# Rotary half heads exchanged by transfers instead of TensorE, and a down projection that waits by groups

## The chip, the cores and the metric

The program runs on one core of one Trainium2 chip. The metric is the time of one execution on the device in microseconds (us). The kernel before took 3718.03 us, the median of three runs (3717.81 to 3725.36).

Engines are named as the profile names them: PE is TensorE (matrix products), DVE is VectorE, ACT is ScalarE, POOL is GpSimd, SP is SyncE, which here only starts transfers.

## The reference

Sequence length and width are 1024. Two attention layers (the first block) are followed by one layer of another kind (the second block).

```
h = layer(layer(x))            # 1st block: 4 branches of 256 columns each
  a: banded attention, band of 8 chunks of 64, relative bias
  b: latent attention: q, k from rms-normed low-rank projections; 64 plain + 32 rotary dims per head
  c: banded attention, band of 2 chunks; q (4 heads) and k (2 heads) of 64 dims, all rotary
  m: attention to a memory of 256 tokens
  y = concat(branch * silu(gate)) @ w_out;  h = layernorm(alpha*x + y)
x = x + 0.5 * swiglu(rmsnorm(x))            # 2nd block: D_FF = 2816 = 22 tiles of 128
x = x + mixer(rmsnorm(x))
x = x + 0.5 * swiglu(rmsnorm(x))

rope(x):   x1, x2 = split(x, 2)             # the two halves of a head
           [x1*cos - x2*sin, x2*cos + x1*sin]
swiglu(h): g, u = split(h @ w_gu, 2);  (silu(g) * u) @ w_down
```

So a rotary tile needs, beside itself, a copy in which the halves of every head are exchanged. Tiles here lie features by tokens (128 partitions by 1024 columns), so the exchange moves data between partitions, which an elementwise engine does not do inside one operation on 128 partitions.

## The kernel before, in words

**Products.** A projection of 128 output features is a *panel*: SP loads 512 KB of float32 weights (`panel_raw`), POOL splits them into a float16 and a bfloat16 part (`panel_parts`, lines 823 to 825), and PE forms each product of 128x128 by 128x512 as three matmuls (lines 1026 to 1028). Attention scores, transposes and values are plain float32 matmuls, as is the exchange of halves. Each float32 matmul shows as two records.

**Attention layers.** A layer is 48 *slots*: 16 of branch a, 8 of c, 16 of b, 8 of m. Slot n on PE is: scores of slot n+1 (L1196 to L1207), fill 0, transposes (L1219), fill 1, transposes (branches with two groups), fill 2, values of slot n (L1238), fill 3. A fill takes the next steps of a list of dense pieces (`LAYER_FILL`), spread evenly over the four fills of all slots of a branch; one step is one product of 128x512. A position is written `at` = 4 x slot + fill: branch a has 0 to 63, c 64 to 95, b 96 to 159. Meanwhile DVE takes the row maxima of slot n+1, ACT its exponentials, DVE the inverse of the sums, POOL scales the rows (L859), and ACT and DVE copy the transposes out of PSUM (L1543, L1956). Each engine runs its own program in order, at the same positions: `keep_layer(at)` on ACT and DVE empties the PSUM banks of the pieces that end there, `layer_background` on DVE holds the rest (the rms norm chain `normalise`, from two positions after `ss_kv`, and the rotary tables). Dense pieces alternate between two PSUM banks (`dense_ready`, `dense_free`), so PE begins a piece only when the last but one is copied out.

**The exchange.** Ten dense pieces per layer, `swap_cq0`, `swap_cq1`, `swap_ck` (end of branch a), `swap_q` and `swap_k` (middle of branch c), two halves of 512 columns each, multiply the tile by a 128x128 permutation with signs (`swap`, L1077). For each half DVE runs `rotate`: the product from PSUM times sin, the tile times cos, and their sum. After `swap_q` and `swap_k` DVE also copies the 32 rotary rows of each head beside its plain rows (L2016 and L2022, seven copies). The scores of c wait for `rope_c_done`, those of b for `rope_b_done`.

**Feed-forward.** `ffn` runs twice. Eleven turns of four tiles form gate and up; DVE and ACT make each activation tile and DVE splits it (`act_split` counts 22). Then eight tiles of the down projection each sum three groups of 8, 8 and 6 activation tiles (`FF_GROUPS`). Before the first, PE waits once for all 22 (L1341).

## Time and profile before

| | |
|---|---|
| median of the runs | 3718.03 us |
| profiled execution, its own time | 3720.31 us |
| its span | 3718.5 us |
| PE busy in the span | 3462.1 us (93%) |
| DVE, ACT, POOL busy | 1544.2, 1002.5, 1573.3 us |
| mean granted PE clock | 0.978 of full |
| share of PE in the chain that ended last | 85% |

The profile is of one execution. A row of the timeline gives the start, the duration, the engine, the line, the operation with output and inputs, a count, and in brackets the idle time of the engine before it with what ended that. PE's matmuls overlap in the records: back to back 128x512 float16 products start 0.216 us apart at full clock and are shown as 0.38 us long. The two attention layers come first, and the second feed-forward ends the program.

### The profile page before, as it was taken

Reading aid. Unit: us, or ns where it says so; the run is one execution under the profiler, and the core shown is the slowest. Engines: PE = TensorE matmul, PEld = TensorE weight load, DVE = VectorE, ACT = ScalarE, POOL = GpSimd, SP = SyncE. Lnnn points to the kernel's source line nnn. Section 1 sums busy time; section 2 is a strip of 40 time slices with the busy share of each in tenths; the row PEclk is TensorE's granted clock in tenths of the full one; section 3 lists DMA queues with packets and bytes.
Section 4 is the critical chain, followed back from the end, with each engine's and each line's share of the span. In section 5 each row is a group of like instructions: output and inputs, shape, how many; then the busy total and the mean of one; then the engine's idle time right before and its main releaser. Section 6 shows DMA issues by size and latency. Waiting matters only on the chain.

```text
span 3718.5 us, 50039 instructions
## 1 busy us (share of the span) xinstructions
PE 3462.1 (93%) x20022; PEld 1785.2 (48%) x20340; DVE 1544.2 (42%) x2435; ACT 1002.5 (27%) x1744; POOL 1573.3 (42%) x1034
## 2 busy tenths in 40 slices
PE   7988997998999799999987999999998979999999
PEld 4554653645564344444434554555544434444444
DVE  3255347145436733331115455545554463333100
ACT  1433322233332300000002455554554320000000
POOL 4444652444564233332324555645554423333232
PEclk9999999998999999999999999999999999999999
DMA  3100112110021111111121101111011111111112
GB/s 121 41 19 35 60 60 83 46 33 32 23 85 36 34 51 51 51 51 47 52 72 73 47 28 48 48 46 48 27 48 72 45 34 52 50 51 51 48 48 80
DMA packets 52885, 188.33 MB, mean 51 GB/s; under 512 B 6624, under 2 KB 7136, under 8 KB 52192
## 3 DMA queue, kind: packets, MB, share of 16 engines
q1 hardware_dynamic: 51408, 181.08, 13.9%
q10 hardware_dynamic: 1296, 4.72, 0.3%
q8 instruction: 128, 2.10, 0.2%
q14 instruction: 53, 0.43, 0.0%
HBM read 173.20 MB, written 12.58 MB: 50 GB/s over the span
## 4 chain that ended last, share of the span: by engine, by line
PE 85%; DVE 5%; ACT 5%; issue 3%; POOL 1%; DMA 1%; SPq 0%; DVEq 0%; POOLq 0%; ACTq 0%
PE pair L1028 25%; PE pair L1026 24%; PE pair L1027 21%; PE pair L1238 3%; PE pair L1207 2%; PE pair L1460 2%; PE pair L1219 2%; DVE arena L1884 2%; PE pair L1436 1%; PE pair L1419 1%; ACT arena L1804 1%; POOL panel_parts L825 1%; ACT arena L1636 1%; PE pair L1367 1%; PE pair L1046 1%
## 5 line engine op out<-in xcount | busy, mean ns | idle before, releaser
L1026 PE MATMUL pair<-operand,panel_parts 128*128 128x512 f16 x2816 | 1075.6, 382 | 90.4 <-POOL panel_parts L825 61.3
L1028 PE MATMUL pair<-operand,panel_parts 128*128 128x512 f16 x2816 | 1071.7, 381 | 12.2
L1027 PE MATMUL pair<-operand,panel_parts 128*128 128x512 bf16 x2584 | 984.4, 381 | 0.0
L824 POOL TENSOR_SCALAR panel_parts<-panel_raw 128x1024 f16<-128x1024 f32 (+3 forms) x287 | 296.0, 1031 | 1568.1 <-PE pair L1028 1054.5
L825 POOL TENSOR_TENSOR panel_parts<-panel_raw,panel_parts 128x1024 bf16<-128x1024 f32 (+3 forms) x287 | 633.7, 2208 | 23.9
L1026 PE MATMUL pair<-arena,panel_parts 128*128 128x512 f16 (+1 forms) x1216 | 464.4, 382 | 41.1 <-DVE arena L1884 29.6
L1026 PEld LDWEIGHTS pair<-operand,panel_parts 128*128 128x128 f16 x2816 | 276.0, 98 | 440.1 <-issue 143.2
L859 POOL TENSOR_SCALAR arena<-arena,row_inv 128x256 f32<-128x256 f32 (+7 forms) x256 | 338.6, 1335 | 344.2 <-DVE row_inv L1946 343.9
L1028 PE MATMUL pair<-arena,panel_parts 128*128 128x512 f16 (+1 forms) x1216 | 463.7, 381 | 5.4 <-issue 1.1
L1028 PEld LDWEIGHTS pair<-operand,panel_parts 128*128 128x128 bf16 x2816 | 276.7, 98 | 336.5 <-issue 7.2
L1027 PE MATMUL pair<-arena,panel_parts 128*128 128x512 bf16 (+1 forms) x1130 | 429.8, 380 | 0.0
L1027 PEld LDWEIGHTS pair<-operand,panel_parts 128*128 128x128 f16 x2816 | 276.7, 98 | 287.8 <-issue 9.0
L976 POOL TENSOR_SCALAR arena<-arena,row_inv 128x512 f32<-128x512 f32 (+1 forms) x128 | 246.9, 1939 | 184.6 <-DVE row_inv L2411 184.6
L1884 DVE TENSOR_TENSOR arena<-arena 128x1024 f32<-128x1024 f32 (+4 forms) x183 | 233.6, 1276 | 79.6 <-ACT arena L1797 49.3
L1715 ACT ACTIVATE arena<-arena 128x1024 f32<-128x1024 f32 x44 | 46.5, 1057 | 756.7 <-DVE arena L1884 756.7
L1636 ACT ACTIVATE arena<-arena,neg_max 128x256 f32<-128x256 f32 (+7 forms) x256 | 155.8, 609 | 344.6 <-DVE neg_max L1927 344.3
L1884 DVE TENSOR_TENSOR arena<-pair,arena 128x1024 f32<-128x1024 f32 (+2 forms) x64 | 67.6, 1056 | 372.2 <-PE pair L1028 367.2
L1026 PEld LDWEIGHTS pair<-arena,panel_parts 128*128 128x128 f16 x1216 | 119.6, 98 | 206.8 <-issue 46.3
L1887 DVE SCALAR_TENSOR_TENSOR residual<-pair,residual 128x1024 f32<-128x1024 f32 (+1 forms) x32 | 39.1, 1221 | 421.6 <-PE pair L1028 421.4
L1927 DVE CUSTOM_DVE_ANT_0 arena<-pair,arena 128x256 f32<-128x256 f32 (+7 forms) x256 | 133.7, 559 | 192.0 <-PE pair L1207 114.7
L1543 ACT ACTIVATE arena<-pair 128x512 f32<-128x512 f32 (+1 forms) x234 | 136.2, 588 | 281.3 <-PE pair L1028 161.1
L1028 PEld LDWEIGHTS pair<-arena,panel_parts 128*128 128x128 bf16 x1216 | 120.2, 99 | 144.0 <-issue 6.9
(213 smaller groups left out, 4241.4 us busy)
## 6 DMA issues: line engine op xcount, KB each, us to landing
panel_raw<-in_wgu SPq DMA_DIRECT2D x88, 512.0 KB, 3.2
panel_raw<-in_wl SPq DMA_DIRECT2D x58, 512.0 KB, 3.2
panel_raw<-in_wm SPq DMA_DIRECT2D x56, 512.0 KB, 3.3
panel_raw<-in_wdn SPq DMA_DIRECT2D x32, 512.0 KB, 3.2
residual_spill<-residual SPq DMA_DIRECT2D x16, 512.0 KB, 2.9
residual<-residual_spill SPq DMA_DIRECT2D x15, 512.0 KB, 5.9
panel_raw<-in_wl SPq DMA_DIRECT2D x18, 384.0 KB, 2.9
panel_raw<-in_wdn SPq DMA_DIRECT2D x16, 384.0 KB, 2.9
```

Of the source, the lines that this page charges most:

```text
L824: chained(nc.gpsimd.tensor_scalar(WP[:, s, 0, 0:cols], RAW[:, s, 0:cols], HI_MAX, -HI_MAX, ALU.min, ALU.max))
L825: nc.gpsimd.tensor_tensor(WP[:, s, 1, 0:cols].bitcast(LO), RAW[:, s, 0:cols], WP[:, s, 0, 0:cols], ALU.subtract).then_inc(panel_split[s], 1)
L859: nc.gpsimd.tensor_scalar(p, p, RI[:, b:b + 1], None, ALU.mult).then_inc(slot_scaled, 1)
L976: nc.gpsimd.tensor_scalar(p, p, RI[:, b:b + 1], None, ALU.mult).then_inc(mix_scaled, 1)
L1026: nc.tensor.matmul(out, stat[0], mov[0], start=first, stop=False)
L1027: nc.tensor.matmul(out, stat[0], mov[1], start=False, stop=False)
L1028: return nc.tensor.matmul(out, stat[1], mov[0], start=False, stop=last)
L1238: m = nc.tensor.matmul(OUTL[u.h * HD:(u.h + 1) * HD, (i // 2) * P:(i // 2 + 1) * P], v_of(s, u, kt), PTL[g][:, c0:c0 + P], start=j == 0, s ...
L1543: return nc.scalar.activation(dst, src, ACT.Copy, scale=scale)
L1636: nc.scalar.activation(p, p, ACT.Exp, bias=NM[:, b:b + 1], scale=-1.0, accum_out=RS[:, b:b + 1]).then_inc(slot_probs, 1)
L1884: return V_.tensor_tensor(out, a, b, op)
L1927: m = V_.tensor_tensor_reduce(out=probs_of(n, s, u), in0=score_cols(s, u), in1=bias_of(s, u), scale=-1.0, scalar=3e38, op0=ALU.add, op1=AL ...
```

## The change

The ten exchange pieces leave PE's list. Instead ACT, after it has copied the second half of a rotary tile, issues transfers that write the exchanged rows to a second tile (`SWAPPED`): four of 32 rows for each of `cq0`, `cq1`, `ck`, two of 16 rows for the key (`bq1`), eight of 16 rows for the query (`ur`). The sign is now a per-partition scale in the sine table. DVE rotates in three whole-width steps at three successive positions, the first three positions after the piece ends (`ROPE_WAIT`). SP issues seven transfers of 32 rows in place of DVE's seven copies, ahead of the panels of branch b. The remaining pieces are spread anew over the fills: 198 steps in place of 204 over branch a, 52 in place of 56 over branch c. In the feed-forward PE waits before each group for that group's activation tiles alone.

```diff
 LAYER_FILL = {
-    "a": [..., "cq0", "ss_q", "ss_kv", "cq1", "ck", "swap_cq0", "swap_cq1", "swap_ck", "cv", "cg0"],
-    "c": ["ur", "un0", "un1", "cg1", "swap_q", "swap_k", "uk0", "uk1", "uv0", "uv1", "bg0"],
+    "a": [..., "cq0", "ss_q", "ss_kv", "cq1", "ck", "cv", "cg0"],
+    "c": ["ur", "un0", "un1", "cg1", "uk0", "uk1", "uv0", "uv1", "bg0"],
+ROPE_WAIT = (("bq1", 3), ("cq0", 3), ("cq1", 3), ("ck", 3), ("ur", 3))
...
+        SWAPPED = {"cq0": GATES[4], "cq1": GATES[5], "ck": GATES[6], "bq1": GATES[7], "ur": GATES[7]}
+        ROTATED = {"cq0": CQ[0], "cq1": CQ[1], "ck": CK, "bq1": BRAW_K, "ur": UR}
...
 # SP, after the load of mem and before the panels of branch b
+                sp.wait_ge(kv_split, l + 1)
+                sp.wait_ge(rope_k_rotated, l + 1)
+                for h in (0, 2, 3):
+                    sp.dma_start(BK[h][64:96], BK[1][64:96]).then_inc(rope_b_done, 16)
+                sp.wait_ge(rope_q_rotated, l + 1)
+                for h in range(4):
+                    sp.dma_start(BQ[h][64:96], UR[32 * h:32 * h + 32]).then_inc(rope_b_done, 16)
...
 # PE, feed-forward
-                pe.wait_ge(act_split, FT * idx)
                 with pe.Fori(0, 2) as i:
...
                             w = weights(f"down{idx}", i, 3 * j + g)
+                            pe.wait_ge(act_split, FT * (idx - 1) + k0 + nk)
...
 # ACT, keep_layer
+                    if name in SWAPPED and c == 1:
+                        layer_piece_kept(act, name, l)
+                        w = 32 if name[0] == "c" else 16
+                        rows = slice(64, 96) if name == "bq1" else slice(0, P)
+                        if name == "ur":
+                            act.wait_ge(rope_k_rotated, l + 1)
+                        for r in range(rows.start, rows.stop, 2 * w):
+                            for a, b in ((r, r + w), (r + w, r)):
+                                nc.scalar.dma_start(SWAPPED[name][a:a + w], ROTATED[name][b:b + w]).then_inc(swap_loaded[name], 16)
...
 # ACT, rotary tables
-                nc.scalar.activation(sin, sin, ACT.Sin).then_inc(rope_tab, 1)
+                nc.scalar.activation(sin, sin, ACT.Sin, scale=RC[:, 4 + n:5 + n]).then_inc(rope_tab, 1)
...
 # DVE
+            def rotate(l, name, step):
...
+                if step == 0:
+                    dve.wait_ge(rope_tab, 2)
+                    dve.wait_ge(swap_loaded[name], (l + 1) * 16 * {"bq1": 2, "ur": 8}.get(name, 4))
+                    chained(tt(other, other, sin[rows], ALU.mult))
+                elif step == 1:
+                    chained(tt(x, x, cos[rows], ALU.mult))
                 else:
+                    tt(x, x, other, ALU.add).then_inc({"bq1": rope_k_rotated, "ur": rope_q_rotated}.get(name, rope_c_done), 1)
...
 # DVE, layer_background, ahead of normalise
+                for name, wait in ROPE_WAIT:
+                    step = at - kept_at(l, name) - wait
+                    if 0 <= step < 3:
+                        rotate(l, name, step)
```

On PE, in slot 13 of layer 1 (the last rows of piece `ck`, then the exchange of `cq0`, `cq1`, `ck`, with the transposes of the slot between), before:

```order
L1026 MATMUL pair<-operand,panel_parts 128x512
L1027 MATMUL pair<-operand,panel_parts 128x512
L1028 MATMUL pair<-operand,panel_parts 128x512
L1077 MATMUL pair<-arena,swap 128x512 [waits dense_free1,dense_free0] x2
L1219 MATMUL pair<-ident,arena 128x128 [waits slot_kept0,slot_scaled]
L1219 MATMUL pair<-ident,arena 128x128 x3
L1219 MATMUL pair<-ident,arena 128x128 [waits slot_kept1]
L1077 MATMUL pair<-arena,swap 128x512 [waits dense_free1,dense_free0] x4
L1219 MATMUL pair<-ident,arena 128x128 [waits slot_kept0,slot_scaled]
```

Now, at the same transposes, the end of `ck` and the first rows of `cv`:

```order
L1220 MATMUL pair<-ident,arena 128x128 [waits slot_kept0,slot_scaled]
L1220 MATMUL pair<-ident,arena 128x128 x3
L1220 MATMUL pair<-ident,arena 128x128 [waits slot_kept1]
L1036 MATMUL pair<-operand,panel_parts 128x512
L1037 MATMUL pair<-operand,panel_parts 128x512
L1038 MATMUL pair<-operand,panel_parts 128x512
```

The six exchange pieces with their waits on both PSUM banks are gone, and ordinary steps stand there. On DVE in the same slot, after the row maxima (`ISA`), before (`rotate` in six-row groups, one step of the norm chain in between):

```order
L1884 TENSOR_TENSOR arena<-pair,arena 128x512 [waits dense_ready0,rope_tab]
L1884 TENSOR_TENSOR arena<-arena 128x512
L1884 TENSOR_TENSOR arena<-arena 128x512 [waits dense_free0,dve_step]
L1884 TENSOR_TENSOR arena<-pair,arena 128x512 [waits dense_ready1,rope_tab,dve_step]
L1884 TENSOR_TENSOR arena<-arena 128x512
L1884 TENSOR_TENSOR arena<-arena 128x512 [waits dense_free1,dve_step]
L1887 SCALAR_TENSOR_TENSOR residual<-residual,layer_cols 128x1024
L1956 COPY stats<-pair 128x128 [waits slot_values,slot_turned1]
L1946 RECIPROCAL row_inv<-row_sum 128x1 [waits slot_probs] x2
```

Now, from the end of slot 12 (the rotation of `cq1` starts there) into slot 13:

```order
L1894 TENSOR_TENSOR arena<-arena 128x1024 [waits swap_loaded_cq1,rope_tab]
L1897 SCALAR_TENSOR_TENSOR residual<-residual,layer_cols 128x1024 [waits cols_loaded,dve_step]
L1937 ISA arena,neg_max<-pair,arena 128x640 [waits slot_scores]
L1937 ISA neg_max 128x1
L1937 ISA arena,neg_max<-pair,arena 128x640
L1937 ISA neg_max 128x1
L1894 TENSOR_TENSOR arena<-arena 128x1024
L1897 SCALAR_TENSOR_TENSOR residual<-residual,layer_cols 64x1024 [waits dve_step]
L1966 COPY stats<-pair 128x128 [waits slot_values,slot_turned1]
L1956 RECIPROCAL row_inv<-row_sum 128x1 [waits slot_probs] x2
```

One whole-width operation of a rotation stands at each position, beside one step of the norm chain, and none reads PSUM. On ACT at the start of branch c, where `ur` is copied out, the eight transfers stand between those copies and the copies of `un0`:

```order
L1544 ACTIVATE arena<-pair 128x512 [waits slot_values,dense_ready0]
L1544 ACTIVATE arena<-pair 128x512 [waits dense_ready1]
L1635 DMA arena<-arena 16x1024 [waits rope_k_rotated,dense_free1,dense_free0]
L1635 DMA arena<-arena 16x1024 x7
L1544 ACTIVATE residual<-pair 64x512 [waits kv_split,dense_ready0]
```

## Rows read from the trace of the kernel before

**Rows 1.** The page: busy time by engine.
```profile
PE 3462.1 (93%) x20022; PEld 1785.2 (48%) x20340; DVE 1544.2 (42%) x2435; ACT 1002.5 (27%) x1744; POOL 1573.3 (42%) x1034
```

**Rows 2.** Windows: us, busy (x) of PE, PEld, DVE, ACT, POOL; clock, DMA.
```profile
60.00:258.70 198.70, 190.78 (x1349) 109.02 (x1363) 83.21 (x196) 73.02 (x146) 93.53 (x60) 0.98 0.09 31
258.70:352.60 93.90, 74.77 (x437) 40.66 (x445) 46.22 (x145) 36.24 (x101) 42.30 (x38) 0.87 0.10 34
```

**Rows 3.** One of PE's waits, whole span: total us, times, longest.
```profile
PE pair L1077 <- DVE arena L1884: 10.9, 10, 2.3
```

**Rows 4.** The exchange line: count, ns min/median/max, first and last start.
```profile
L1077 PE MATMUL pair<-arena,swap x32: 592/595/1222, 213.1 to 910.9; 128*128 128x512 f32 x32
```

**Rows 5.** Timeline of PE, layer 1, slot 13, the exchange for branch c.
```profile
213.15 1.02 PE L1077 MATMUL pair<-arena,swap 128*128 128x512 f32 x2
...
222.25 2.08 PE L1077 MATMUL pair<-arena,swap 128*128 128x512 f32 x2 [2.32 <-DVE arena L1884]
...
226.35 1.27 PE L1219 MATMUL pair<-ident,arena 128*128 128x128 f32 x5
...
230.92 1.31 PE L1238 MATMUL pair<-stats,arena 128*64 128x128 f32 x20 [0.92 <-DVE stats L1956]
```

**Rows 6.** Timeline of DVE there.
```profile
214.89 3.14 DVE L1884 TENSOR_TENSOR arena<-arena 128x512 f32<-128x512 f32 x2
...
218.67 1.41 DVE L1884 TENSOR_TENSOR arena<-arena 128x512 f32<-128x512 f32 x2
...
232.47 1.22 DVE L1884 TENSOR_TENSOR arena<-residual,arena 128x1024 bf16<-128x1024 f32 x1
```

**Rows 7.** Timeline of POOL there.
```profile
214.62 2.13 POOL L825 TENSOR_TENSOR panel_parts<-panel_raw,panel_parts 128x1024 bf16<-128x1024 f32 x1
```

**Rows 8.** Timeline of PE, layer 1, branch c, values of slots 18 to 21.
```profile
290.34 1.09 PE L1238 MATMUL pair<-stats,arena 128*64 128x128 f32 x16 [1.15 <-ACT stats L1543]
...
292.76 0.93 PE L1207 MATMUL pair<-arena 64*128 64x128 f32 x8
...
298.59 1.09 PE L1238 MATMUL pair<-stats,arena 128*64 128x128 f32 x16 [0.68 <-ACT stats L1543]
...
313.56 0.61 PE L1026 MATMUL pair<-arena,panel_parts 128*128 128x512 f16 x1 [4.45 <-DVE arena L1884]
...
315.64 1.55 PE L1238 MATMUL pair<-stats,arena 128*64 128x128 f32 x12 [0.62 <-issue]
...
326.76 0.23 PE L1026 MATMUL pair<-panel_parts,arena 128*128 128x128 f16 x1 [3.68 <-ACT residual L1543]
...
330.94 1.09 PE L1238 MATMUL pair<-stats,arena 128*64 128x128 f32 x16
```

**Rows 9.** Timeline of DVE there: the gate of a piece.
```profile
301.82 0.69 DVE L1887 SCALAR_TENSOR_TENSOR arena<-arena,pair 128x512 f32<-128x512 f32 x1 [1.68 <-ACT arena L1580]
```

**Rows 10.** Timeline of ACT, start of branch c: copies of `ur`, then of `un0`.
```profile
264.79 1.06 ACT L1543 ACTIVATE arena<-pair 128x512 f32<-128x512 f32 x2
269.46 1.20 ACT L1543 ACTIVATE residual<-pair 64x512 f32<-64x512 f32 x2 [3.61 <-PE pair L1028]
```

**Rows 11.** ACT's transfers of x: issue in ns (min/median/max), landing.
```profile
L1539 ACTq DMA_DIRECT2D residual<-in_xT x8: 347/454/511, 0.7 to 8.4; - x8
...
DMA to landing us min/median/max: 5.5/9.9/17.1
```

**Rows 12.** The smallest transfer inside the program: KB, us to landing.
```profile
column_mask<-in_cmask SPq DMA_DIRECT2D x1, 32.0 KB, 1.8
```

**Rows 13.** Timeline of PE, first feed-forward, into the down projection.
```profile
1708.31 0.60 PE L1026 MATMUL pair<-arena,panel_parts 128*128 128x512 f16 x1 [6.74 <-DVE arena L1884]
...
1712.98 0.42 PE L1028 MATMUL pair<-arena,panel_parts 128*128 128x512 f16 x1
```

**Rows 14.** Timeline of POOL there: the split of the second down panel.
```profile
1702.89 3.18 POOL L825 TENSOR_TENSOR panel_parts<-panel_raw,panel_parts 128x1024 bf16<-128x1024 f32 x1
```

**Rows 15.** Timeline of PE, second feed-forward, into the down projection.
```profile
3483.75 0.60 PE L1026 MATMUL pair<-arena,panel_parts 128*128 128x512 f16 x1 [6.74 <-DVE arena L1884]
```

More of the change, by code:

```diff
@@ L203, in piece_steps @@
         return [(0, 4)]
-    if name[:4] == "swap" or name[:2] in ("uk", "uv") or name == "ss_kv":
+    if name[:2] in ("uk", "uv") or name == "ss_kv":
         return [(c, 1) for c in range(2)]
@@ L234, in layer_tables @@
                 ends.setdefault(at, []).append((name, l, c))
-                if name[:4] == "swap" or name[:2] == "ss":
+                if name[:2] == "ss":
                     continue
@@ L391, in build @@
         ones = sb("ones", [P, P])
-        swap = sb("swap", [P, 2, P])
         LC = sb("layer_cols", [P, LAYERS, NL_COLS])
@@ L397, in build @@
         DECA = sb("decay_all", [P, 8, 4])
-        RC = sb("rope_cols", [P, 4])
+        RC = sb("rope_cols", [P, 6])
         negsink = sb("negsink", [P, 2, 4])
@@ L514, in build @@
         rope_c_done = sem("rope_c_done")
+        swap_loaded = {x: sem(f"swap_loaded_{x}") for x in SWAPPED}
+        rope_k_rotated, rope_q_rotated = sem("rope_k_rotated"), sem("rope_q_rotated")
         mem_split = sem("mem_split")
@@ L684, in constants @@
             def constants():
-                for dst, name in ((ident, "ident"), (RC, "rope_cols"), (ones, "ones"), (swap, "swap"), (SC, "scols"),
+                for dst, name in ((ident, "ident"), (RC, "rope_cols"), (ones, "ones"), (SC, "scols"),
                                   (MCA, "mcols"), (head_ones, "head_ones")):
@@ L702, in layer_panels @@
                     name = PIECE_PANEL.get(name, name)
-                    if name[:4] != "swap" and name[:2] != "ss" and name not in done:
+                    if name[:2] != "ss" and name not in done:
                         done.append(name)
@@ L1068, in layer_piece @@
                         nc.tensor.matmul(dst, ones[0:64], BSQ[1][0:64, cc], start=False, stop=True).then_inc(done, 1)
-                    yield
-                    return
-                if name[:4] == "swap":
-                    src = {"swap_cq0": CQ[0], "swap_cq1": CQ[1], "swap_ck": CK, "swap_q": UR, "swap_k": BRAW[1]}[name]
-                    layer_piece_kept(pe, {"swap_q": "ur", "swap_k": "bq1"}.get(name, name[5:]), l)
-                    if name == "swap_k":
-                        pe.wait_ge(kv_split, l + 1)
-                    which = swap[:, 0 if name[5] == "c" else 1]
-                    nc.tensor.matmul(dst, which, src[:, cc], start=True, stop=True).then_inc(done, 1)
                     yield
@@ L1565, in keep_layer @@
                     cc = slice(c * HALF, (c + 1) * HALF)
-                    if name[:4] == "swap" or name[:2] == "ss" or name[0] == "o":
+                    if name[:2] == "ss" or name[0] == "o":
                         continue
@@ L1966, in _ @@
             gates_seen = [0]
-            def rotate(x, piece, cos, sin, rows, done):
-                name, l, c = piece
-                cc = slice(c * HALF, (c + 1) * HALF)
-                src, free = layer_piece_ready(dve, piece)
-                d = LPIECE[piece]
-                tt(SWAPPED[rows, cc], src[rows], sin[rows, cc], ALU.mult).then_inc(free, 1)
-                chained(tt(x[rows, cc], x[rows, cc], cos[rows, cc], ALU.mult))
-                dve.wait_ge(free, d // 2 + 1)
-                m = tt(x[rows, cc], x[rows, cc], SWAPPED[rows, cc], ALU.add)
-                if done is not None and c == 1:
-                    m.then_inc(done, 1)
-                else:
-                    chained(m)
-                return m
+            def rotate(l, name, step):
+                wide = name[0] == "c"
+                rows = slice(64, 96) if name == "bq1" else slice(0, P)
+                cos, sin = (COS64, SIN64) if wide else (COS32, SIN32)
+                x, other = ROTATED[name][rows], SWAPPED[name][rows]
+                if step == 0:
[4 more added lines that the diff above has]
+                    chained(tt(x, x, cos[rows], ALU.mult))
+                else:
+                    tt(x, x, other, ALU.add).then_inc({"bq1": rope_k_rotated, "ur": rope_q_rotated}.get(name, rope_c_done), 1)
             def keep_layer(at):
@@ L2615, in constants @@
     f32 = (10000.0 ** (-np.arange(0, 32, 2) / 32)).astype(np.float32)[p % 16]
-    swap = np.zeros((P, 2, P), np.float32)
-    for n, w in enumerate((64, 32)):
-        src = (p // w) * w + (p % w + w // 2) % w
-        swap[src, n, p] = np.where(p % w < w // 2, -1.0, 1.0)
+    sign = [np.where(p % w < w // 2, -1.0, 1.0) for w in (64, 32)]
     cs = np.clip(p % GRID - 8, 0, GRID - 16)[:, None]
@@ L2624, in constants @@
     return {
-        "ident": np.eye(P, dtype=np.float32), "ones": np.ones((P, P), np.float32), "swap": swap,
-        "rope_cols": np.stack([f64, f32, np.full(P, np.pi / 2), np.zeros(P)], axis=1).astype(np.float32),
+        "ident": np.eye(P, dtype=np.float32), "ones": np.ones((P, P), np.float32),
+        "rope_cols": np.stack([f64, f32, np.full(P, np.pi / 2), np.zeros(P), *sign], axis=1).astype(np.float32),
         "cmask": cmask, "head_ones": (p[:, None] // HD == p[None, :] // HD).astype(np.float32),
```

34 lines of the change are left out of this document (8 added, 26 removed), and 1 row of the table LAYER_FILL.

## The prediction

> **What bounds the kernel now.** I read the page first: PE is busy for 3462.1 us, no other engine for half of the span [rows 1]. So work taken from PE, and waits of PE, are what can be won. Then the two stretches of a layer that the change touches. In branch a (60 to 258.7 us) PE is busy 190.78 of 198.7 us at 0.98 of the clock, so it sets the pace. In branch c (258.7 to 352.6) it is busy 74.77 of 93.9 us at 0.87: here 19 us per layer are idle, and the clock drops as well [rows 2]. Next PE's waits: the exchange line alone waits 10.9 us for DVE over ten waits [rows 3]. Last the timelines around the exchange and at the start of the down projection. The reader is to see there that the exchange is serial: one half fills a bank, DVE empties it, sums, and only then has the next half its bank.
>
> I work with the profiled execution, 3720.31 us (span 3718.5, with 1.8 around it). The median is 2.3 us less; I carry the saving over to it.
>
> **Term 1, the exchange in branch a.** Per layer PE loses three names in two halves. Their products alone are small: 32 records over both layers for the four tiles in the arena [rows 4], at 0.51 each (a pair takes 1.02 [rows 5]), some 16 us. What stands on the path is the whole stretch from 213.15 to 226.35, 13.2 us, since PE does nothing else in it but the five transposes of slot 13, which stay (about 0.55) [rows 5]. That leaves 12.65. The stretch also leaves a slow clock behind. A pair of exchange records takes 1.02 us at its start and 2.08 us after the wait of 2.32; the next transposes take 1.27; that is the level of 1.2 in place of 2.4 GHz. I give 0.8 us for the work done at the low level behind 226.35. Then the values of slot 13 wait 0.92 for DVE's backlog [rows 5]. Upper bound: 12.65 + 0.8 + 0.9 = 14.4 us.
>
> What comes in its place: DVE gets three operations of 128x1024 per name, each at least 1.22 us [rows 6], at positions where the norm chain also puts one. Over slots 11, 13 and 14 that is three, two and three rotary steps beside three, four and two of the chain. In slot 13: six times 1.22, row maxima 2 x 0.83, and about 1 us of copies, inverses and gate, some 10 us in a slot of about 11.5. It fits, with about 1.5 us left, but the small DVE copies that PE's values wait for now stand behind up to 2.5 us of background. I charge 1.4 us per layer. ACT issues four transfers after the last copy of each name; issuing took 0.454 us each in the only ACT rows [rows 11], so 1.8 us. Behind them on ACT stand the copies of transposes for the same slot, which have about 3 us. I charge nothing; if that cover goes, it is under 1 us for each of three names. The last rotary step of `ck` is at position 58, PE asks for it at 60: a slot's half, some 5 us. Term 1: 14.4 - 1.4 = **13 us per layer**, 26 in all. Bounds 9.5 and 14.4 per layer.
>
> The lower bound is also what a port conflict would leave. Two operations of 128x512 from SBUF took 3.14 us while POOL's split of 2.13 us ran [rows 7], and 1.41 us without it [rows 6]; so one met conflict costs 1.7 us. The Trainium skill ("SBUF — State Buffer", section "SBUF: two separate sides") says that a VectorE operation with two SBUF inputs and a GpSimd operation that reads SBUF exclude each other for the whole instruction. By that rule the change makes things worse in kind, since all three operations of a rotation now have two SBUF inputs, where one in three read PSUM; the trace's 3.14 against 1.41 agrees.
>
> **Term 2, the exchange in branch c.** The values of slots 18 and 19 are 8.25 us apart. From there to slot 20, which holds the exchange, it is 17.05, and to slot 21 another 15.30 [rows 8]. So slots 20 and 21 take 32.35 us against 16.5 for two plain ones. The largest wait, 4.45 us at 313.56, is for DVE, which runs `rotate` and the seven copies there. All that goes. But 15.85 is an upper bound, because the pieces `uk` and `uv` move into slot 20 and have their own waits. Two things stay late:
> - `uk0`'s second half takes the bank of the second half of `cg1`, which now ends one fill before it and is not emptied until ACT has done slot 21's exponentials and DVE the gate. In a plain slot ACT is through at about the time of the values, 5.8 us behind the scores (292.76 to 298.59) [rows 8]. With ACT's 0.6 and DVE's 0.69 for the gate [rows 9] and one step of 0.65 the values come about 1.9 us late: slot 20 takes 10.1.
> - the wait of 3.68 us at 326.76 for ACT's copies [rows 8] remains, at 2.2 to 3.7.
> And after each such wait the clock is low for some microseconds, worth up to 2 us per slot. So 12 for slot 20 and 12 for slot 21, 24 of the 32.35. Term 2: **8.5 us per layer**, 17 in all; bounds 4 and 15.85 per layer.
>
> In the other six slots nothing is won although they carry half a step less: there PE waits at the values for ACT (1.15 and 0.68 us [rows 8]), so the chain scores, maxima, exponentials, copy sets the length and a lighter fill only lengthens that wait.
>
> The eight transfers for `ur` cost ACT 8 x 0.454 = 3.6 us from 265.85 on. ACT was idle just there for 3.61 us until the first product of `un0` [rows 10], so it is hidden to the last tenth. If it were not, `un0`'s copies move by the excess, and PE, which waits for ACT's copies once in each of slots 16 and 17, by as much: 0.5 us at 511 ns per issue.
>
> **Transfers.** DVE waits for the exchanged rows three positions, at least 8 us in branch a (three fourths of a slot of 11.5) and 6 in c, less 2.4 us for copy and issue. No row shows a transfer within SBUF of 64 or 128 KB. Bounds: 1.8 us, the 32 KB load [rows 12], and 17.1 us, the last of eight 512 KB loads started together [rows 11]. I take 2.5, near the small one, since little else is in flight. Then no wait appears. The Trainium skill ("DMA: Bandwidth & Descriptors", section "Rules for kernel authors") says that under 64 KB one pays mostly overhead and that small transfers should be joined; here 22 transfers a layer stand for five. Its fixed cost of about 2 us would, as an estimate, also stay within the three positions.
>
> SP's seven transfers wait for the query's rotation, one or two positions after the point where SP already waited (the end of `un1`). Behind them stand the panels of branch b. The first of these is split only when `uv1` is done, fifteen positions on. Nothing. The sign as a scale, the lost constant and the fewer DVE copies (already in term 2) cost nothing.
>
> **Term 3, the down projection.** PE waits 6.74 us before the first product, then runs at half clock: starts 0.43 us apart until 1712.98 [rows 13], 11 products that would take 0.216 each, so 2.3 us. The second feed-forward shows the same 6.74 [rows 15]. With the wait by groups PE goes on at once: the first group reads tiles 0 to 7, long split; its panel is split one tile earlier. The second group starts 48 x 0.216 = 10.4 us later, and its panel is ready when POOL's split ends at 1706.07 [rows 14], 4.5 us into the first. The last tile's split ended 6.7 us in, and the group that reads it starts at 20.7. So all 9.05 us go, **18 in all**; bounds 13.5 (the wait alone) and 18.1.
>
> **Sum.** 26 + 17 + 18 = 61. 3720.3 - 61 = 3659; against the median 3718 - 61 = **3657 us**.
>
> **Rivals.**
> 1. *Everything goes*, no new wait in c and none in a: 14.4 x 2 + 15.85 x 2 + 18.1 = 78.6, so 3639. For it speaks that the before shows how much a wait costs beyond itself (clock); against it, PE's waits for ACT in c in slots without any exchange. Chance 0.13.
> 2. *Branch c keeps its length*: the freed time turns into waits of `uk` and `uv` for their banks, since ACT reaches them only behind the exponentials. Term 2 is 0: 3674. Chance 0.12.
> 3. *DVE and POOL collide in branch a*: eight rotary steps a layer stand in slots 11, 13 and 14; if each meets a POOL operation at 1.7 us, that is 13.6, less some 4.5 of room, 9 a layer: 3657 + 18 = 3675. For it: POOL is busy 93.53 of 198.7 us in this stretch [rows 2]. Against: only about half the steps can meet one. Chance 0.12.
> 4. *Late landings*, the slower side. DVE takes its work in order, so a wait for the exchanged rows holds the next row maxima, and PE with them. There are ten such waits. Each has 6 us behind the issue and about 5 us of room in the slot chain, so a landing of 11 us costs nothing and each microsecond beyond it ten. The saving of 61 is gone at 17.1 us, which is the worst row [rows 11]; at 20 us it is 3657 + 90 = 3747. Against it stand 1.8 us [rows 12]. Chance 0.04.
> 5. *The down projection gains nothing*, because another wait (bank, panel) ends as late as the one removed. Against it: the first group's panel and bank are free before PE's last tile of gate and up ends. 3657 + 18 = 3675. Chance 0.04.
>
> My forecast has 0.55. Its own range is 3648 to 3667. With rivals 1 to 3 and 5 at its edges the range for 8 in 10 is 3639 to 3679. A change under 0.2% (7.4 us) can't be told from none. Faster by more: all cases but the fourth, less some for what I have not seen: 0.93; within: 0.03; slower: 0.04.
>
> **What would show it.** In the changed profile: no product with `swap`; slot 13's values 11 to 13 us behind those of slot 12; DVE steps with `swap_loaded` waits of no length; the values of slot 20 10 to 12 us behind slot 19, with a wait of 1 to 3 us at the second half of `uk0`; slot 21 at 11 to 13. The first product of each down projection directly behind the last of gate and up, at full clock. It is wrong if DVE shows idle time ended by a transfer, if the values of slots 11 to 14 wait more than 1 us each for DVE's copies, or if slot 20 stays above 14 us.

## The result and the profile after

The changed kernel takes 3686.2 us (median of 4 runs, 3680.0 to 3687.9); the kernel before, beside it, 3719.6 (3717.8 to 3725.4). The ratio is 0.9908, 95% interval 0.9897 to 0.992. So it is faster by 33 us where 61 were forecast (3657, range 3639 to 3679). The direction was right, the size was not: the time lies outside the range.

The profiled execution took 3687.64 us, span 3685.9 against 3718.5. First the page, busy time by engine, against [rows 1]:

```profile
PE 3437.9 (93%) x19978; PEld 1777.1 (48%) x20300; DVE 1535.9 (42%) x2391; ACT 1002.3 (27%) x1744; POOL 1578.6 (43%) x1034
```

PE lost 24.2 us of work and the span 32.6, so PE's idle time fell by only 8.4 us (256.4 to 248.0), although the two waits of 6.74 before the down projections and the 10.9 of the exchange line are gone: some 16 of these 24 us came back elsewhere. The windows of branch a and of branch c (from the values of slot 15 on) show where, against [rows 2]:

```profile
60.00:248.84 188.84, 178.68 (x1304) 103.63 (x1319) 88.55 (x189) 73.31 (x146) 98.47 (x60) 1.00 0.14 41
248.84:350.23 101.39, 82.89 (x497) 46.93 (x505) 41.13 (x139) 39.48 (x107) 50.60 (x41) 0.88 0.20 51
```

In branch a PE stands idle for 10.2 us, more than the 7.9 of [rows 2] in a longer stretch, although the exchange and its waits are gone. PE's waits of the whole span name the new ones (total us, times, longest), against [rows 3]:

```profile
PE pair L1239 <- issue: 17.9, 22, 2.9
PE pair L1220 <- ACT stats L1544: 12.5, 6, 2.3
...
PE pair L1239 <- ACT stats L1544: 9.1, 6, 2.0
...
PE pair L1036 <- DVE arena L1897: 6.3, 2, 3.2
```

L1220 is the transposes, L1239 the values, L1544 ScalarE's copy out of PSUM. The kernel before has no wait for ScalarE at the transposes; here there are six, three a layer. From here on slot n means the stretch from the values of slot n-1 to the values of slot n; only the pair that is called "slots 16 and 17" is counted otherwise (see below). The timeline of PE has the three waits of layer 1 in slots 9, 11 and 12:

```profile
169.29 0.41 PE L1220 MATMUL pair<-ident,arena 128*128 128x128 f32 x2 [1.83 <-ACT stats L1544]
...
195.60 0.63 PE L1220 MATMUL pair<-ident,arena 128*128 128x128 f32 x4 [2.33 <-ACT stats L1544]
...
209.16 0.74 PE L1220 MATMUL pair<-ident,arena 128*128 128x128 f32 x5 [2.10 <-ACT stats L1544]
```

And the timeline of ScalarE shows what stood ahead of that copy each time:

```profile
165.93 1.06 ACT L1689 ACTIVATE residual<-residual 128x1024 f32<-128x1024 f32 x1
...
191.67 1.28 ACT L1695 ACT_TABLE_LOAD   x1
192.97 2.00 ACT L1695 ACTIVATE residual<-residual 128x1024 f32<-128x1024 f32 x2
194.88 0.58 ACT L1544 ACTIVATE stats<-pair 128x512 f32<-128x512 f32 x1
...
205.88 2.44 ACTq L1635 DMA_DIRECT2D arena<-arena  x4
208.42 0.60 ACT L1544 ACTIVATE stats<-pair 128x512 f32<-128x512 f32 x1 [2.63 <-issue]
```

At slot 9 it is the three squares of 1.05 us, at slot 11 the inverse roots with their table load (3.3 us), at slot 12 the four issues for `cq1`, which ends in the first fill of that slot (position 48). The issues were forecast at 0.454 us each and with three microseconds of room. The squares and roots are no part of the diff. They stand behind `kept_at("bkv")` and `kept_at("ss_kv") + 1`. With six steps fewer in branch a (198 in place of 204) these positions went from 35 to 36 and from 43 to 44: out of the last fill of a slot, where ScalarE has nothing urgent, into the first of the next, between the exponentials and the copy that PE's second transposes need.

The transfers, by line (ns min/median/max to issue, then us to landing), against [rows 11]:

```profile
L1635 ACTq DMA_DIRECT2D arena<-arena x40: 514/612/1277, 179.7 to 865.0; - x40
...
DMA to landing us min/median/max: 2.2/2.3/3.0
```

They land as assumed (2.5), and no VectorE wait on them appears. The Trainium skill ("DMA: Bandwidth & Descriptors", section "Anatomy of one DMA — SWDGE (gpsimd) path") puts the fixed cost of a transfer that GpSimd issues at about 2.0 us; the 2.3 measured here, for transfers that ScalarE issues, is near it. Issuing is a third dearer than assumed (0.612 against 0.454). The eight of `ur` take 5.67 us and hold the first copies of `un0` (timeline of ScalarE), against [rows 10]:

```profile
260.00 5.67 ACTq L1635 DMA_DIRECT2D arena<-arena  x8
265.77 1.20 ACT L1544 ACTIVATE residual<-pair 64x512 f32<-64x512 f32 x2 [5.84 <-PE pair L1038]
```

PE does wait for ScalarE's copies of `un0` soon after, and then, in slot 20, for VectorE:

```profile
271.99 0.39 PE L1036 MATMUL pair<-arena,panel_parts 128*128 128x512 f16 x1 [1.62 <-ACT residual L1544]
...
304.30 0.61 PE L1036 MATMUL pair<-arena,panel_parts 128*128 128x512 f16 x1 [3.16 <-DVE arena L1897]
```

The first row looks like the price of the issues; issue_on_sync below shows that it isn't. The last row is the wait of the second half of `uk0` that the prediction named. Windows from the values of slot 15 to those of 16, and so on to 19, give a granted clock of 0.77 and 0.72 from the values of 16 to those of 18 (the expectations and the text below call these two windows "slots 16 and 17"). A clock of 1.00 is TensorE's upper level of 2.4 GHz and 0.50 its lower of 1.2. The second fence shows where it falls: in the 2.9 us that PE waits before the values of 16, ahead of `ur`'s first issue at 260.00.

```profile
248.84:260.51 11.67, 8.68 (x59) 4.49 (x59) 5.17 (x19) 4.00 (x13) 5.46 (x5) 0.95 0.14 46
260.51:273.08 12.57, 10.63 (x48) 5.45 (x50) 5.84 (x19) 5.65 (x16) 5.58 (x5) 0.77 0.26 43
273.08:285.21 12.13, 10.30 (x49) 5.39 (x51) 5.64 (x18) 4.51 (x13) 6.08 (x6) 0.72 0.61 153
285.21:294.88 9.67, 7.52 (x53) 4.23 (x54) 3.72 (x17) 2.92 (x11) 2.90 (x5) 1.00 0.29 68
```

```profile
258.50:259.00 0.50, 0.00 (x0) 0.00 (x0) 0.23 (x2) 0.50 (x4) 0.50 (x1) 1.00 0.88 360
...
259.50:260.00 0.50, 0.00 (x0) 0.00 (x0) 0.47 (x2) 0.43 (x1) 0.50 (x1) 0.50 0.00 0
```

The last of the four windows, slot 19, is at full clock and still 1.4 us longer than before (9.67 against 8.25). ScalarE and then VectorE show the same thing there as in branch a: the gate of `cg1` stands between the exponentials and the copies that PE's values wait for.

```profile
292.27 0.58 ACT L1581 ACTIVATE arena<-pair 128x512 f32<-128x512 f32 x1
292.75 0.58 ACT L1544 ACTIVATE stats<-pair 128x512 f32<-128x512 f32 x1
```

```profile
292.96 0.69 DVE L1897 SCALAR_TENSOR_TENSOR arena<-arena,pair 128x512 f32<-128x512 f32 x1 [2.58 <-ACT arena L1581]
...
294.09 0.69 DVE L1966 COPY stats<-pair 128x512 f32<-128x512 f32 x1
```

The first half of `cg1` ends at position 76 now and ended at 75 before (52 steps in place of 56): again from the last fill of a slot into the first of the next. PE's wait at these values is 2.10 us; before it was 0.68 [rows 8].

The down projection begins as forecast: the first product stands 0.22 us behind the last of gate and up, and the starts stay 0.215 us apart, full level, against [rows 13]:

```profile
1684.71 0.38 PE L1038 MATMUL pair<-operand,panel_parts 128*128 128x512 f16 x1
1684.93 0.38 PE L1036 MATMUL pair<-arena,panel_parts 128*128 128x512 f16 x1
1685.14 0.38 PE L1037 MATMUL pair<-arena,panel_parts 128*128 128x512 bf16 x1
```

### The profile page after: what moved, and what is told of

It is laid out like the page before. It is cut to its first block, busy times and chain, and to the rows that moved or that the text cites. A ratio compares the mean times of both kernels' runs of the same rounds, so it can differ in the third digit from the quotient of the medians.

```text
span 3685.9 us, 49988 instructions
## 1 busy us (share of the span) xinstructions
PE 3437.9 (93%) x19978; PEld 1777.1 (48%) x20300; DVE 1535.9 (42%) x2391; ACT 1002.3 (27%) x1744; POOL 1578.6 (43%) x1034
## 4 chain that ended last, share of the span: by engine, by line
PE 67%; ACT 4%; issue 2%; DVE 2%; POOL 1%; DMA 0%; SPq 0%; DVEq 0%; POOLq 0%; ACTq 0%
PE pair L1038 20%; PE pair L1036 20%; PE pair L1037 18%; PE pair L1461 2%; PE pair L1437 1%; PE pair L1208 1%; PE pair L1239 1%; PE pair L1420 1%; ACT arena L1814 1%; PE pair L1368 1%; POOL panel_parts L835 1%; ACT L1794 1%; PE pair L1220 1%; PE pair L1421 0%; ACT arena L1778 0%
## 5 line engine op out<-in xcount | busy, mean ns | idle before, releaser
L835 POOL TENSOR_TENSOR panel_parts<-panel_raw,panel_parts 128x1024 bf16<-128x1024 f32 (+3 forms) x287 | 636.3, 2217 | 23.9
L1894 DVE TENSOR_TENSOR arena<-arena 128x1024 f32<-128x1024 f32 (+4 forms) x177 | 241.0, 1362 | 79.7 <-ACT arena L1807 49.9
L1544 ACT ACTIVATE arena<-pair 128x512 f32<-128x512 f32 (+1 forms) x234 | 136.1, 588 | 288.8 <-PE pair L1038 168.0
L1894 DVE TENSOR_TENSOR arena<-pair,arena 128x1024 f32<-128x1024 f32 x44 | 53.9, 1225 | 371.8 <-PE pair L1038 367.2
```

The lines of the kernel that those rows point to most:

```text
L835: nc.gpsimd.tensor_tensor(WP[:, s, 1, 0:cols].bitcast(LO), RAW[:, s, 0:cols], WP[:, s, 0, 0:cols], ALU.subtract).then_inc(panel_split[s], 1)
L1544: return nc.scalar.activation(dst, src, ACT.Copy, scale=scale)
L1894: return V_.tensor_tensor(out, a, b, op)
```

## The experiments

Theory 1: the issues on ScalarE cost the missing time. Theory 2: the new spread of the steps does, by where it puts ScalarE's background work and by the clock in branch c. Theory 3: the rotation on VectorE does. The runs come from several sets, each with the kernel before run beside it; the ratio is taken within a set. Each profile gives two lengths a layer: slot 0 to 15 (branch a, term 1) and slot 15 to 24 (branch c, term 2), values to values. Both layers are shown, layer 1 first.

| kernel | 0 to 15 | 15 to 24 | median us | ratio, 95% interval |
|---|---|---|---|---|
| before | 183.6, 183.8 | 106.1, 104.7 | 3717.8 to 3720.8 | 1 |
| forecast | 170.7 | 96.9 | 3657 | |
| changed | 177.5, 177.5 | 101.4, 101.7 | 3686.2 | 0.9908 (0.9897 to 0.992) |
| changed_again | 179.1, 179.1 | 101.7, 98.8 | 3686.7 | 0.9909 (0.9895 to 0.9923) |
| down_alone | 183.6, 183.6 | 102.6, 106.2 | 3702.3 | 0.9956 (0.9943 to 0.997) |
| no_rotation | 178.5, 178.5 | 99.1, 97.2 | 3681.7 | 0.9896 (0.988 to 0.9912) |
| no_transfer | 174.7, 176.3 | 100.5, 101.7 | 3680.3 | 0.9894 (0.9876 to 0.9913) |
| busy_waits | 178.6, 178.6 | 99.0, 95.0 | 3680.3 | 0.9894 (0.9879 to 0.991) |
| issue_on_sync | 174.7, 174.7 | 97.4, 95.6 | 3675.9 | 0.9889 (0.9874 to 0.9905) |
| spread_in_a_only | 176.8, 176.8 | 95.3, 97.5 | 3674.9 | 0.9875 (0.9857 to 0.9894) |
| old_spread | 177.0, 176.9 | 94.5, 94.4 | 3671.0 | 0.9873 (0.9857 to 0.9888) |
| two_steps | 173.1, 173.1 | 96.9, 97.0 | 3671.1 | 0.9869 (0.9854 to 0.9883) |
| spread_and_sync | 176.3, 176.3 | 95.6, 95.5 | 3670.2 | 0.9868 (0.985 to 0.9887) |
| two_steps_and_sync | 170.3, 170.3 | 95.6, 99.8 | 3666.2 | 0.9864 (0.985 to 0.9879) |
| best_of_both | 170.3, 170.3 | 97.4, 97.7 | 3659.4 | 0.9837 (0.9824 to 0.985) |

The second column is the same in both layers, no_transfer excepted, but differs by 1.6 us between the two profiles of the changed kernel. That is the clock: in both, PE waits 2.33 us in slot 11, and only in changed_again does it fall behind that wait, to half for about three microseconds. Slot 11 then takes 15.15 us and not 13.76. no_rotation (15.0) and layer 2 of no_transfer (14.9) have the same fall.

```profile
186.13:201.28 15.15, 12.77 (x63) 6.09 (x64) 9.79 (x14) 7.88 (x11) 5.04 (x2) 0.91 0.11 36
```

The third column moves by up to 4 us within one profile, with the clock, and shows only differences larger than that. Single slots at full clock repeat to 0.1 us and say more.

**down_alone.** The kernel before plus the line `pe.wait_ge(act_split, FT * (idx - 1) + k0 + nk)` in the group loop, less the wait ahead of it.

> The kernel before with only the new waits of the down projection. My term 3 says 18.1 us below before (9.05 each): about 3700.5. Its rival, that another wait ends as late, says no change. If less than 15 us go, part of the 28 us that are missing from the forecast of 61 stands here; if 18 go, all of it stands in the exchange (terms 1 and 2).

15.5 us at the medians, interval 11 to 21, which holds the 18.1. The traces give it more closely. Stretches in us, from the sum of one norm to that of the next (the second feed-forward: to its last product), and in the last row from the values of layer 1's slot 24 to those of layer 2's slot 0:

| stretch | before | down_alone | changed | changed_again | best_of_both |
|---|---|---|---|---|---|
| first feed-forward | 669.4 | 660.2 | 660.2 | 660.2 | 660.2 |
| mixer | 1106.0 | 1107.9 | 1108.1 | 1110.5 | 1105.4 |
| second feed-forward | 664.7 | 655.8 | 655.7 | 655.7 | 655.8 |
| between the layers' branches | 318.8 | 320.7 | 321.8 | 319.8 | 318.8 |

The two down projections give 9.2 and 9.0 us: term 3 holds, and most of the missing time is in the exchange. The other two rows move by 3 to 5 us from profile to profile, in down_alone too, whose exchange is untouched.

**issue_on_sync.**

```diff
-                                nc.scalar.dma_start(SWAPPED[name][a:a + w], ROTATED[name][b:b + w]).then_inc(...)
+EXCHANGE_AHEAD = {"ck": "bq1", "cg0": "cq0", "uq": "cq1", "cg1": "ck"}   # ur: behind the panels of branch c
+                        if name in EXCHANGE_AHEAD:
+                            exchange(l, EXCHANGE_AHEAD[name])             # the same transfers, by sp.dma_start
                         layer_panel(l, name)
```

> The changed kernel, but SyncE issues the 22 exchange transfers of a layer, each name's ahead of the panel it would load next, and ScalarE none. Theory 1 (issuing costs: 0.61 us each in place of 0.454, in order ahead of ScalarE's copies of transposes) expects the waits of 2.1 us at slot 12 and 1.6 us after ur to go, and some of slots 13 and 14: 3.5 to 5 us a layer, 7 to 10 in all below the changed kernel, about 3677. Theory 2 (the spread of the pieces over the fills moved ScalarE's squares and roots ahead of its copies) expects at most 2 us.

Some 10 us below the changed kernel at the medians; the intervals of the two ratios overlap a little, the stretches of branch a don't. The issues take SyncE about as long as they took ScalarE (0.59 us), but nothing waits behind them. In ScalarE's timeline at slot 12 the two copies now follow one another:

```profile
205.04 0.57 ACT L1558 ACTIVATE arena<-pair 128x512 f32<-128x512 f32 x1
205.52 0.58 ACT L1558 ACTIVATE stats<-pair 128x512 f32<-128x512 f32 x1
```

Branch a gains 2.8 us: 1.9 in slot 12 (`cq1`), 0.9 in slot 13 (`ck`), nothing in slot 10 (`cq0`). Branch c gains 4 to 6. All of that is in slots 16 and 17, which need 18.9 us at full clock where they took 24.7:

```profile
257.53:267.41 9.88, 7.94 (x48) 3.99 (x50) 5.81 (x19) 5.65 (x16) 5.58 (x5) 1.00 0.33 55
267.41:276.44 9.03, 7.18 (x49) 4.02 (x51) 5.65 (x18) 4.51 (x13) 6.90 (x6) 1.00 0.63 165
```

The expectation missed here. The wait behind `ur` was to go, and it is still there with the same length, though ScalarE issues nothing (no_transfer has it as well, again 1.62):

```profile
266.32 0.39 PE L1050 MATMUL pair<-arena,panel_parts 128*128 128x512 f16 x1 [1.62 <-ACT residual L1558]
```

The copy that PE waits for stands behind the exponentials, not behind the issues: in the changed kernel the issues end at 265.7 us and ScalarE starts that copy at 270.74, right after the exponentials. In both kernels PE's waits in slots 16 and 17 are the same, and the whole difference of 5.8 us is in its busy time (10.63 and 10.30 against 7.94 and 7.18): it is the clock alone. So `ur`'s issues cost PE no wait that the traces show.

**no_transfer.** No exchange transfers; `tt(other, x, sin[rows], ALU.mult)` in place of `tt(other, other, ...)`.

> The changed kernel without the 22 exchange transfers: the first rotary step multiplies the unexchanged rows, and VectorE waits for ScalarE's copy in place of the transfer. It leaves out the exchange of the half heads. Upper bound of what the transfers cost by issue, landing and traffic together. Theory 1: as with the issue on SyncE, 7 to 10 us below the changed kernel, and the two within 3 us of one another. Theory 2: at most 2 us below the changed kernel.

A miss: it is 6 us below the changed kernel and not 7 to 10, and 4 above issue_on_sync, though it has no transfer at all. Branch a agrees in layer 1 (174.7); layer 2 has the fall of the clock in slot 11 (176.3). In branch c slots 16 and 17 had a clock of 0.85 and 0.84 in layer 1, and the five runs spread from 3670.9 us (mean clock 0.983) to 3687.9 (0.978). ScalarE's work no longer differs from issue_on_sync, and the times follow the clock, so the spread is most likely the clock's.

**old_spread.**

```diff
-    "a": [..., "ss_q", "ss_kv", "cq1", "ck", "cv", "cg0"],
+    "a": [..., "ss_q", "ss_kv", "cq1", "ck", "gap_0", "gap_1", "gap_2", "cv", "cg0"],
-    "c": ["ur", "un0", "un1", "cg1", "uk0", ...],
+    "c": ["ur", "un0", "un1", "cg1", "gap_3", "gap_4", "uk0", ...],
+                        if name[:3] == "gap":
+                            yield
```

> The changed kernel, but the ten fill steps of the exchange stay in the tables as empty steps, so every other piece keeps the position it had before and squares and roots stand in the last fill of their slot again; PE does no more work. Theory 2 expects the waits of 1.83 (slot 9) and 2.33 us (slot 11) to go, 4 us a layer, and branch c to lose its extra waits, 1 to 3 us a layer: 10 to 14 us below the changed kernel, about 3673. Theory 1 expects no change (within 3 us), or a loss, since PE has less to do in two slots and waits there.

15 us below the changed kernel, but not where the theory put it: 0.5 us a layer in branch a (2.2 against changed_again) and 7 in branch c (4 to 7). Slots 9 and 11 are again as before (10.3 and 10.9 us), and so is slot 19 (8.25). Slot 13, where all six empty steps stand, takes 16.1 us, since nothing lies beside its chain of maxima, exponentials, issues and copies:

```profile
221.83 1.30 PE L1223 MATMUL pair<-ident,arena 128*128 128x128 f32 x5 [5.35 <-ACT stats L1550]
```

**spread_and_sync**, both edits.

> The changed kernel with both: the ten fill steps kept as empty steps, and all transfers issued by SyncE. Against the changed kernel the one gave 15 and the other 10 us. If they remove different waits (slot 12 and the transfers of ur by the one, slots 9 and 11 and the low clock of slots 16 and 17 by the other) branch a takes 173 us in place of 177.5 and 174.7 and the whole about 3665 to 3668. If both work only by the clock of slots 16 and 17, which is at full level with either of them, the combination adds nothing: 3671.

The 173 for branch a did not come: it is 176.3, 0.6 below old_spread. Moving the issues gives 0.2 us in slot 10 and 0.8 in slot 13, which at 15.3 us stays long because it is empty; slot 14 loses 0.4, and slot 12 had no wait for them left, since `cq1` ends in a last fill here (position 47). The whole, 3670.2, is nearer to the second figure, but slots 16 and 17 are not at full clock (20.4 and 20.5 us against 19.6 in old_spread), so the reason given with it isn't shown.

**spread_in_a_only**, the first three gaps alone.

> The changed kernel with the six empty steps in branch a alone; branch c keeps the thinner fills. From slot 0 to slot 15 as with all ten (176.9 us), slots 16 and 17 at full clock (19.5 us). If the fills of branch c matter too, slots 15 to 24 take 97 to 98 us where all ten empty steps give 94.5, and the whole is 3676; if only the clock at the entry of branch c matters, they take 95 and the whole is 3671.

Branch c takes 95.3 and 97.5 us, one layer for each of the two answers, and the whole (3674.9) is nearer to the first. Over all of branch c its own fills matter by no more than the clock scatters. In slot 19 they do matter: it takes 9.67 us in every profile with the thinner fills and 8.25 in every one with the fills of the kernel before, at full clock both times. That is 1.4 us a layer, for the third block that the new spread moved. best_of_both and two_steps_and_sync below differ by these fills alone, and in slot 19 by the same 1.4.

**busy_waits.**

```diff
+            def waste(n):
+                pe.wait_ge(slot_gated, n)
+                for _ in range(10):
+                    nc.tensor.matmul(OUTL[:], XH[:, 0:P], XH[:, 0:2 * P], start=True, stop=True)
```

> The changed kernel with waste work on PE (ten products of 128x128x256, some 1.1 us, whose result is overwritten) put where PE stands waiting: before the second transposes of slots 11 and 12 and before the values of slots 15, 16 and 17. It adds 11 us of PE work in two layers. If a wait costs itself and no more, it is no faster than the changed kernel: 3686 to 3694. If the lower clock after the waits is the cost (slots 16 and 17: 24.7 us at 0.77 and 0.72 here, 18.9 us at 1.0 in the kernel whose transfers SyncE issues), it is faster: slots 16 and 17 in 20 us, 3676 to 3680.

11 us more work on PE, and the kernel is not slower (3680.3, at the edge of the second answer and outside the first). Slots 16 and 17 take 20.0 us in both layers, at full clock:

```profile
260.40:271.38 10.98, 9.19 (x60) 4.90 (x60) 6.58 (x19) 6.10 (x16) 6.35 (x5) 1.00 0.29 48
271.38:280.40 9.02, 7.23 (x51) 4.00 (x51) 4.88 (x18) 3.95 (x12) 5.92 (x6) 1.00 0.65 167
```

In the two profiles of the changed kernel they took 24.7, 25.0, 23.0 and 20.5 us. That fits the clock as a cost of its own, but the intervals of the two ratios overlap: the whole time does not show it.

**no_rotation.** Without steps 0 and 1 of `rotate`, step 2 on 8 columns.

> The changed kernel with the transfers, but without the first two of VectorE's three operations of each rotation, and the third on 8 columns: it leaves out the rotation. Theory 3 (VectorE's 15 more operations a layer delay its row maxima and copies, alone or by meeting GpSimd's splits) expects 6 us a layer or more to come back, under 3672. Theories 1 and 2 expect at most 3 us in all, 3683 to 3688.

Branch a takes 178.5, which is 0.6 less than changed_again, the profile with the same fall of the clock in slot 11; all of it is in slot 14 (11.9 against 12.5). Theory 3 wanted 6 and is out. The Trainium skill ("SBUF — State Buffer", section "SBUF: two separate sides") says that a VectorE operation with two SBUF inputs and a GpSimd operation that reads SBUF exclude each other for the whole instruction. Nothing here contradicts it, but its price is small. The nine 128x1024 operations of this form between 130 and 260 us in the changed kernel take 1325 ns in the mean, against the 1.22 us of [rows 6]; GpSimd's two scalings in slot 11 take 5.03 us beside them and 3.74 without, and PE's only wait in that slot is for ScalarE.

```profile
L1894 DVE TENSOR_TENSOR arena<-arena 128x1024 f32<-128x1024 f32 x9 | 11.9, 1325 | 0.0
```

**two_steps_and_sync.** issue_on_sync with one gap of two empty steps in branch a: with 200 steps squares and roots stand at positions 35 and 43 again.

```diff
-    "a": [..., "ck", "cv", "cg0"],
+    "a": [..., "ck", "gap_0", "cv", "cg0"],
```

> The kernel whose transfers SyncE issues, with two empty fill steps in branch a (200 steps in place of 198), which are just enough to put ScalarE's squares and roots back into the last fill of slots 8 and 10; branch c keeps its fills. In that kernel slots 9 and 11 still take 1.4 and 2.8 us more than before. If these come from the position of squares and roots, branch a (slot 0 to slot 15) falls from 174.7 to 170.5 us, which is my forecast for term 1, and the whole from 3675.9 to about 3667. If the thinner fills are the cause, two steps do not change it: 174 us and 3675.

Branch a takes 170.3 us, within 0.4 of term 1. Against issue_on_sync that is 4.4 less, and slots 9 and 11 alone give it (1.6 and 2.8). The waits at the transposes shrink to (whole span):

```profile
PE pair L1236 <- ACT stats L1563: 0.9, 4, 0.2
```

**two_steps**, with the issues on ScalarE.

> The changed kernel, its transfers issued by ScalarE, with the same two empty steps. If the 7 us that branch a lacks of the forecast are 4.2 for squares and roots and 2.8 for the issues, it takes 173.3 us (177.5 in the changed kernel), and the whole is 8 us shorter, or up to 18 if slots 16 and 17 come to full clock as well: 3668 to 3678. If issues and positions only matter together, more than 175.

173.1 us. The two causes add up: 4.4 for the positions (177.5 to 173.1), 2.8 for the issues (to 170.3). Only the sums do, for the two steps also move the ends of `cq0` (41 to 40) and `cq1` (48 to 47), so that the issues now cost 1.1 us in slot 10 and 1.7 in slot 13. Against changed_again, with its fall of the clock in slot 11, the positions are worth 6.0.

**best_of_both.**

> SyncE issues, two empty steps in branch a, four in branch c (so that c has the fills of the kernel before). Branch a 170.5 and branch c 94.5 us, as in the parts measured before: 6.4 us a layer less than with all ten empty steps and ScalarE's issues (3671), so 3658. If a shorter wait in one place only comes back in another, it is level with the best so far: 3668 to 3671.

3659.4 us: 59 us below before, 27 below the changed kernel. Branch a is as expected; branch c in the profile (3665.0, the slowest of the five) is 97.4 and 97.7 and not 94.5. Slots 16 and 17 have the low clock again (0.85 and 0.84 in layer 1), with neither issues nor moved blocks on ScalarE. The other four runs took 3656.7 to 3660.3 at a mean clock of 0.984 to 0.985, 0.982 in the profiled one.

**changed_again.**

> The changed kernel as it is, to have its time on the same chip as the others of this set: 3680 to 3688 us at a mean clock between 0.983 and 0.980, as in its four first runs, with the shorter ones at the higher clock.

3676.3 to 3691.4 us, wider than expected, and again ordered by the clock at its ends (0.984 and 0.978).

## Why the prediction was wrong

Of 61 us, 28 did not come. By the two profiles: 13.5 in branch a, 9.2 in branch c, 2.9 between branch c of layer 1 and the next layer, 2.0 in the mixer, the rest in pieces under 1.

*Term 1 (13 a layer; 6.2 measured, 4.6 in the second profile)* failed at two steps. "I charge nothing" for the issues, because ScalarE's copies "have about 3 us": the copy behind them is the one that frees the bank of PE's second transposes. It is also the one that the exponentials already make late, so there is no room; and an issue takes 0.61 us, not 0.454. That is 2.8 us a layer. The price named for this case ("under 1 us for each of three names") was right in its sum (1.9, 0.9 and 0), and was left out of the term. The larger step is one that the prediction does not have at all: removing pieces changes the spread of all others over the fills. I looked at what moves on PE and VectorE and not at ScalarE's two blocks that hang on piece positions. That is 4.4 us a layer, 6.0 where the clock falls behind the wait. With both undone the stretch is 170.3 us against 170.7 forecast, so the sum of 12.65 + 0.8 + 0.9 - 1.4 stands. Its terms were not measured apart. The 1.4 for VectorE's backlog looks too high: no_rotation gives 0.6 a layer back.

*Term 2 (8.5; 4.7 and 3.1 measured, 4.4 and 6.0 in the second profile).* (32.35 less 24 is 8.35; the sum carried 8.5.) The two slots with the exchange came out near the 24 forecast: slots 20 and 21 together take 23.6 and 25.2 us, 25.6 and 26.8 in the second profile, with the wait for `uk0` where it was put. The step that failed is "in the other six slots nothing is won": it left out that something can be lost. Three things were. Slot 19 is 1.4 us longer in every profile, since the new spread put the gate of `cg1` ahead of ScalarE's copy: the same unseen step as in term 1. Slots 16 and 17 ran at 0.77 and 0.72 of the clock and took 24.7 and 25.0 us, where they took 23.9 and 22.4 before and take 18.9 at full clock. And slots 22 and 23 lost 1.9 in layer 1, again at a lower clock (0.86 in slot 23). `ur`'s issues, which were to be hidden in 3.61 us and took 5.67, are not among them: PE's waits are the same without them. With issue_on_sync branch c is 97.4 and 95.6 long, where 97.6 and 96.2 were forecast; but what it gains there is clock. That the issues bring the low clock is not shown: it falls before the first of `ur`'s, the kernel without transfers had it too, so had best_of_both, and so had the kernel before (0.75 and 0.87 in layer 1). What tips it stays open.

*Term 3 (18)* was right: the wait and the half clock behind it went in both down projections, 9.2 and 9.0 us.

*The rivals.* The landings of the fourth are excluded (at most 3.0 us). So is the third, the collisions: without the rotation branch a is 0.6 us shorter and not 9. So is the fifth, by down_alone. The second, that branch c keeps its length, has half of its price but not its mechanism: the waits at `uk0` (3.2 us) and for ScalarE's copies in slot 21 (2.9 us) stood in the forecast, and what came on top are slot 19 and the clock. My range ended at 3679, worked out from one rival at a time; the issues, the spread and the clock failing together were not in it.

*Left open,* beside the clock of slots 16 and 17: the 2.9 us between the layers and the 2.0 in the mixer. down_alone, in which the exchange is as before, has 1.9 of each, and the two profiles of the changed kernel differ by 2.0 and 2.4 there. So single profiles scatter by about as much as is missing; they don't show that the exchange has a part in it.

## What to carry to other kernels

Where a table spreads work over slots, removing an item moves everything that is keyed to the table, on engines that the change does not touch: list those positions before and after, and look at what stands first in the slot's chain. Here three blocks of ScalarE moved by one position each, and cost 5.8 us a layer. A DMA issue is an instruction on its engine, here 0.6 us; put it where nobody waits behind it. A wait that stands right behind a suspect is not yet its price: the 1.62 us behind `ur`'s issues stayed when the issues went. And where waits and clock interact, one profile gives the length of a stretch only to the scatter of the clock, so such a term needs that scatter as its range.

## What the hardware showed that was not expected

Issuing 64 to 128 KB transfers within SBUF took ScalarE's queue 0.514 to 1.277 us each (median 0.612), eight in a row 5.67, and SyncE's about the same (0.590). Landing took 2.2 to 3.0 us for ScalarE's; the seven 128 KB transfers that SyncE starts in one go, in place of VectorE's copies, landed after 6.2 to 6.3 (medians of the two kinds).

The same wait left the clock alone in one profile and halved it in another: 2.33 us in slot 11, 1.00 in the changed kernel (although a wait of 2.10 followed in the next slot), 0.91 over the slot in changed_again. In the same way the first of the two slots 16 and 17 took from 11.4 to 13.9 us with the same instructions and program.
